# Strassen's scheme on eight slabs of the second column group of the down projections

## The chip, the cores and the metric

The kernel runs on one core of one Trainium2 chip. The metric is the device time of one execution in microseconds. TensorE is written PE (its weight loads PEld), VectorE DVE, ScalarE ACT, GpSimd POOL, and SyncE SP; SP only issues transfers here.

## The reference

Two transformer blocks over 256 tokens of width 2048, in float32. The first has a sparse attention and a gated recurrence, the second has two layers, a pooling mixer and a differential attention, and each of these two layers ends in the part that the change touches:

```python
def swiglu(h, w_gate, w_up, w_down):
    return (jax.nn.silu(h @ w_gate) * (h @ w_up)) @ w_down

def second_block(x, ...):
    for l in range(DEPTH_2):          # 2 layers
        ...
        h = rmsnorm(x, norm_ffn_pre[l])
        x = x + rmsnorm(swiglu(h, w_ffn_gate[l], w_ffn_up[l], w_ffn_down[l]), norm_ffn_post[l])
    return x
```

The hidden width is 5632, so that `w_down` is 5632 x 2048.

## The kernel before

**Tiling.** Every projection is cut into slabs of 1 MB of weights: 256 rows (two tiles of 128, `kt` = 2) by 1024 columns (two halves of 512). A stage (`Stage`) goes through its column groups, and in each through its slabs. A down projection (`down0`, `down1`, one per layer) has two column groups (0 and 1) of 22 slabs (0 to 21). The two token tiles and the two halves give four accumulators of 128 x 512 in PSUM, `acc`, with bank number 2t + n.

**Each slab** is fetched by SP in two transfers of 512 KB into one of `RING` = 5 slots of `raw`. ACT rounds it to the shorter format (`hi`, four slots, line 1486), DVE writes what is left (`lo`, line 2098) into the same place as `raw`, and signals `slab_split`. PE then makes three matmuls for each product (hi by hi, hi by lo, lo by hi; lines 808 to 810), 2 x 2 x 2 x 3 = 24 for a slab, and signals `slab_used`.

**Seven products in place of eight.** The slabs named in `SEVEN[g]` (3, 6, 9, 12, 15 in both groups) are multiplied by Strassen's scheme in Winograd's form: a slab is a 2 x 2 block of weights, the gated activations of its two row tiles and two token tiles another. DVE makes four sums of weight blocks (`weight_sums`, lines 2160 to 2163); three of them go into the next slot of the ring, as a slab of its own that nothing is fetched for (`"sums3"` and so on, 1536 columns wide). It also makes sums of the activations (`side_sums`, lines 2236 to 2241), which ACT rounds (`side_hi`) and DVE splits (`side_lo`, line 2246); they are made once, in group 0, and read again in group 1. PE runs 7 x 3 = 21 matmuls (`seven`, lines 1248 to 1250), 12 on the slab itself and 9 on the sums slab, partly into a second set of accumulators, `wk`.

**Mixing.** After the last such slab, DVE combines the four banks of `wk` (`mix_products`, lines 2252 to 2256) ahead of its conversion of slab 18, and adds the results into `acc` (`mix_into_acc`, lines 2263 and 2266) ahead of that of slab 19. For this PE leaves `acc` alone in turn: banks 2 and 3 rest from the end of slab 16 until the second half (t = 1) of slab 17, and banks 0 and 1 from the middle of slab 17 (signal `acc_paused`) until slab 18. PE waits for `acc_loaded` where it comes back.

**Order.** Each engine's program is a list written out by hand. DVE and ACT convert the slabs in the order of the list `slabs`, and SP fetches in that order (`RAWS`): the load of a slab waits until the slab five places earlier in the ring is used. Two transfers stand outside it: `keep_x` parks the residual x in DRAM, since the gate and up stages use its place, and `fetch_x` (line 700, two transfers of 1 MB) brings it back. It stands ahead of the load of slab 3 of group 0 of the down projection and waits for the last paired slab of the up stage. x is needed at the end of the down stage, when the normed result is added to it.

These are the loop that sets the order of the slabs, and the place of the fetch in SP's loop:

```python
            for s in range(2 if paired else 0, st.slabs):
                slabs.append((st, g, s))
                if st in st_down and s in SEVEN[g]:
                    slabs.append((st, g, f"sums{s}"))
...
            if st in st_down and (g, s) == (0, 3):
                fetch_x(st_down.index(st))
```

Of the kernel before, what the change touches and what calls it, by code (L numbers as in the profile page):

```python
# [39 lines left out]
SEVEN = ((3, 6, 9, 12, 15), (3, 6, 9, 12, 15))  # L40
# [56 lines left out]
def build(nc, t_in, out):  # L97
# [25 lines left out]
    SIDES_AT = (A0 + 8, A0 + 12, A0 + 4, A0 + 20, S0 + 1)  # L123
# [188 lines left out]
    for st in (st_rest, st_out, st_pool, st_gu[0], st_down[0], st_k, st_q, st_v, st_o, st_gu[1], st_down[1]):  # L312
        for g in range(st.groups):
            paired = st in st_gu and g >= CHAINED
            if paired:
                slabs += [(st, g, part) for part in "ABCD"]
            for s in range(2 if paired else 0, st.slabs):
                slabs.append((st, g, s))
                if st in st_down and s in SEVEN[g]:
                    slabs.append((st, g, f"sums{s}"))  # L320
# [34 lines left out]
    N_SIDES = len(SEVEN[0])  # L355
# [52 lines left out]
    MIX_DONE = max(SEVEN[0]) + 1  # L408
# [246 lines left out]
    def _(sp):  # L655
# [100 lines left out]
    def _(pe):  # L756

        def product(st, g, s, tokens=range(TT), between=None):
# [18 lines left out]
            for t in tokens:  # L777
                if st in st_down and (s, t) in ((MIX_DONE + 1, 1), (MIX_DONE + 2, 0)):
                    for n in range(2):
                        pe.wait_ge(acc_loaded[st.bank(t, n)], down_loaded(st_down.index(st), g, st.bank(t, n)))  # L780
                pauses = st in st_down and (s, t) in ((MIX_DONE, 1), (MIX_DONE + 1, 0))
                if st.lhs is not gt:
                    pe.wait_ge(h_ready, h_needed(st, k_end, t))
                for n in ([s] if st is st_pool else range(st.halves)):
# [8 lines left out]
                    for kk in range(st.kt):  # L793
# [13 lines left out]
                        loaded = (st.name, g, b) in LOADED or st in st_down and s > MIX_DONE + (t == 0)  # L807
# [429 lines left out]
        def seven(l, g, s):  # L1237

            st, i = st_down[l], SEVEN[0].index(s)
# [12 lines left out]
            first, last = s == min(SEVEN[g]), s == max(SEVEN[g])  # L1252
# [101 lines left out]
        def ffn(l):  # L1354
# [28 lines left out]
            for s in range(st_down[l].slabs - (2, 4)[l]):  # L1383
                down(l, 1, s)
# [78 lines left out]
    def _(act):  # L1463
# [586 lines left out]
    def _(vec):  # L2050
# [782 lines left out]
        def ffn(l):  # L2833
# [31 lines left out]
            for g in range(FG):  # L2865
# [155 lines left out]
    def _(pool):  # L3021
# [60 lines left out]
        pool.wait_ge(slab_used, number["down0", 0, MIX_DONE + 2] + 1)  # L3082
# [29 lines left out]
        pool.wait_ge(slab_used, number["down1", 0, MIX_DONE + 2] + 1)  # L3112
# [26 lines left out]
```

## Time and profile before

| | us |
|---|---|
| median of 3 runs | 2427.58 |
| lowest and highest | 2427.58, 2428.46 |
| the profiled execution, its time | 2428.43 |
| the profiled execution, its span | 2426.6 |
| PE busy | 2384.8 |
| DVE busy | 1973.3 |
| ACT busy | 1299.3 |
| mean granted PE clock | 0.996 |

The span runs from the first to the last instruction of the profile. Busy time is that of one engine, and engines overlap. In a timeline, a row is a group of like instructions one behind the other: its start, its length, the engine and line, the operation with output and input, the count, and in brackets how long the engine had been idle before it and what ended that. "DMA to landing" is the time from the issue of a transfer until its data are there. A matmul's listed length reaches past the start of the next one, because matmuls are pipelined.

### The profile page before, as it was taken

The numbers are of one execution on the slowest core, as the hardware profiler recorded it, in microseconds if no ns is written. First come the engines' busy times: TensorE is split into PE (matmuls) and PEld (weight loads), VectorE is DVE, ScalarE is ACT, GpSimd is POOL, SyncE is SP. The second block draws the span as 40 slices with busy tenths as digits, with TensorE's granted clock in tenths as the row PEclk, the third lists the DMA queues.
The fourth block names the chain that finished last, engine by engine and source line by source line (L and its number), as shares of the span: only waits on it lengthen the run. The fifth ranks groups of instructions, "written<-read, shape, count | busy, mean of one in ns | idle before, by whom it ended". The sixth has DMA issues, their size and how long they took to land.

```text
span 2426.6 us, 28811 instructions
## 1 busy us (share of the span) xinstructions
PE 2384.8 (98%) x11030; PEld 1979.5 (82%) x11030; DVE 1973.3 (81%) x2564; ACT 1299.3 (54%) x1703; POOL 99.0 (4%) x150
## 2 busy tenths in 40 slices
PE   5999999999999999999999999999999999999998
PEld 4888878888888888888888888888888888888887
DVE  6998988766889899897777768965699898988776
ACT  4757765445555555654444544554555555555443
POOL 0210000000000000000000212100000000000000
PEclk8999999999999999999999999999999999999999
DMA  9997665474566566566656655446666565565654
GB/s 383 360 385 246 240 208 171 166 262 167 192 208 208 191 208 196 186 199 215 229 188 205 196 196 193 160 142 203 218 210 200 188 212 188 195 222 189 224 191 156
DMA packets 190649, 515.46 MB, mean 212 GB/s; under 512 B 17920, under 2 KB 18208, under 8 KB 188208
## 3 DMA queue, kind: packets, MB, share of 16 engines
q1 hardware_dynamic: 178160, 465.31, 56.5%
q0 software_dynamic: 11824, 46.14, 5.1%
q8 instruction: 88, 1.44, 0.2%
q10 hardware_dynamic: 528, 2.16, 0.2%
q14 instruction: 49, 0.40, 0.0%
HBM read 507.26 MB, written 6.29 MB: 212 GB/s over the span
## 4 chain that ended last, share of the span: by engine, by line
PE 95%; DVE 2%; SPq 1%; DMA 0%; issue 0%; ACT 0%; DVEq 0%; ACTq 0%
PE acc L808 18%; PE acc L810 17%; PE acc L809 17%; PE acc L1276 4%; PE acc L1275 4%; PE acc L1277 4%; PE wk L1276 4%; PE wk L1275 4%; PE wk L1277 4%; PE acc L1317 1%; PE acc L1316 1%; PE acc L1318 1%; PE wk L1317 1%; PE wk L810 1%; PE wk L809 1%; PE wk L1316 1%
## 5 line engine op out<-in xcount | busy, mean ns | idle before, releaser
L2098 DVE TENSOR_TENSOR lo<-raw,hi 128x1024 fp32r<-128x1024 f32 (+2 forms) x428 | 486.8, 1188 | 110.2 <-ACT hi L1486 108.6
L1486 ACT ACTIVATE hi<-raw 128x1024 fp32r<-128x1024 f32 (+2 forms) x428 | 414.6, 1026 | 253.0 <-PE acc L810 122.1
L2100 DVE SCALAR_TENSOR_TENSOR lo<-raw,gcols,hi 128x1024 fp32r<-128x1024 f32 (+1 forms) x392 | 479.7, 1267 | 50.8 <-ACT hi L1486 48.3
L808 PE MATMUL acc<-hi,h 128*128 128x512 f32 x1312 | 519.4, 396 | 1.5 <-DVE lo L2098 0.5
L810 PE MATMUL acc<-hi,h 128*128 128x512 f32 x1312 | 511.7, 390 | 0.0
L809 PE MATMUL acc<-lo,h 128*128 128x512 f32 x1312 | 511.3, 390 | 0.0
L1486 ACT ACTIVATE hi<-raw,gcols 128x1024 fp32r<-128x1024 f32 (+1 forms) x392 | 416.6, 1124 | 140.4 <-PE acc L810 59.6
L808 PEld LDWEIGHTS acc<-hi,h 128*128 128x128 f32 x1312 | 246.8, 188 | 53.7 <-issue 2.7
L810 PEld LDWEIGHTS acc<-hi,h 128*128 128x128 f32 x1312 | 246.6, 188 | 52.3
L809 PEld LDWEIGHTS acc<-lo,h 128*128 128x128 f32 x1312 | 246.9, 188 | 49.1
L808 PE MATMUL acc<-hi,g_hi 128*128 128x512 f32 x544 | 211.9, 390 | 0.0
L810 PE MATMUL acc<-hi,g_lo 128*128 128x512 f32 x544 | 211.7, 389 | 0.0
L809 PE MATMUL acc<-lo,g_hi 128*128 128x512 f32 x544 | 211.6, 389 | 0.0
L1275 PE MATMUL acc<-hi,h 128*128 128x512 f32 x480 | 186.7, 389 | 0.0
L1276 PE MATMUL acc<-lo,h 128*128 128x512 f32 x480 | 186.7, 389 | 0.0
L1277 PE MATMUL acc<-hi,h 128*128 128x512 f32 x480 | 186.7, 389 | 0.0
L1275 PE MATMUL wk<-hi,h 128*128 128x512 f32 x400 | 155.6, 389 | 0.0
L1276 PE MATMUL wk<-lo,h 128*128 128x512 f32 x400 | 155.6, 389 | 0.0
L1277 PE MATMUL wk<-hi,h 128*128 128x512 f32 x400 | 155.6, 389 | 0.0
L2852 DVE STREAM_TRANSPOSE g_raw<-gated 32x256 f32<-32x256 f32 x320 | 139.4, 436 | 5.3
L810 PEld LDWEIGHTS acc<-hi,g_lo 128*128 128x128 f32 x544 | 102.1, 188 | 21.3
L809 PEld LDWEIGHTS acc<-lo,g_hi 128*128 128x128 f32 x544 | 102.1, 188 | 21.1
(445 smaller groups left out, 3403.8 us busy)
## 6 DMA issues: line engine op xcount, KB each, us to landing
raw<-in_w_ffn_gate SPq DMA_DIRECT2D x176, 512.0 KB, 3.8
raw<-in_w_ffn_up SPq DMA_DIRECT2D x176, 512.0 KB, 4.7
raw<-in_w_ffn_down SPq DMA_DIRECT2D x176, 512.0 KB, 4.7
raw<-in_w_in SPq DMA_DIRECT2D x144, 512.0 KB, 4.8
raw<-in_w_kv SPq DMA_DIRECT2D x64, 512.0 KB, 4.9
ada_raw<-in_ada_w POOLq DMA_DIRECT2D x38, 512.0 KB, 7.2
gate_raw<-in_ada_w POOLq DMA_DIRECT2D x32, 512.0 KB, 6.2
raw<-in_w_out SPq DMA_DIRECT2D x32, 512.0 KB, 4.8
```

The lines of the kernel that those rows point to most:

```text
L808: pe.matmul(o, l_hi, w_hi[:, c], start=first, stop=False, skip_group_check=loaded)
L809: pe.matmul(o, l_hi, w_lo[:, c], start=False, stop=False, skip_group_check=loaded)
L810: mm = pe.matmul(o, l_lo, w_hi[:, c], start=False, stop=last, skip_group_check=loaded)
L1275: pe.matmul(o, l_hi, w_hi, start=False, stop=False, skip_group_check=g >= CHAINED)
L1276: pe.matmul(o, l_hi, w_lo, start=False, stop=False, skip_group_check=g >= CHAINED)
L1277: mm = pe.matmul(o, l_lo, w_hi, start=False, stop=last, skip_group_check=g >= CHAINED)
L1316: pe.matmul(o, lhs[p][0], w_hi, start=first and p == 0, stop=False, skip_group_check=True)
L1317: pe.matmul(o, lhs[p][0], w_lo, start=False, stop=False, skip_group_check=True)
L1486: ins = act.activation(hi[:, m % HI_SLOTS, c], raw[:, r, c], ACT.Copy, scale=scale)
L2098: ins = vec.tensor_tensor(lo[:, r, c], raw[:, r, c], hi[:, m % HI_SLOTS, c], ALU.subtract)
L2100: ins = vec.scalar_tensor_tensor(out=lo[:, r, c], in0=raw[:, r, c], scalar=gcols[:, st.gain, k:k + 1], in1=hi[:, m % HI_SLOTS, c], op0=ALU ...
L2852: ins = vec.transpose(dst, src)
```

## The change

Group 1 of both down projections takes eight slabs by the seven-product scheme (1, 3, 6, 9, 12, 13, 14, 15) instead of five, and its slabs are run in another order, `DOWN_ORDER`, in which such slabs and ordinary ones alternate from position 0 to 15: 0, 1, 2, 3, 4, 6, 5, 9, 7, 12, 8, 13, 10, 15, 11, 14, and then 16 to 21. Group 0 keeps its slabs and order. The side sums of slabs 14, 1 and 13 are made in group 0 beside slabs 18, 20 and 21 (`LATE_SIDES`), and lie where x lies otherwise (`X0`, `X0 + 4`, `X0 + 8`). So `fetch_x` moves from slab 3 of group 0 to slab 17 of group 1, and waits until the sums slab of 14 is used; DVE waits for x later. The places of the mixing become a table (`MIX_AT`): as they were in group 0, and in group 1 the products ahead of the conversion of 17 and the additions ahead of that of 18.

```diff
-SEVEN = ((3, 6, 9, 12, 15), (3, 6, 9, 12, 15))
+SEVEN = ((3, 6, 9, 12, 15), (1, 3, 6, 9, 12, 13, 14, 15))
+LATE_SIDES = {18: 14, 20: 1, 21: 13}
+DOWN_ORDER = (0, 1, 2, 3, 4, 6, 5, 9, 7, 12, 8, 13, 10, 15, 11, 14, 16, 17, 18, 19, 20, 21)
+LAST_SEVEN = (15, 14)
+MIX_AT = ((16, 17, 18, 18, 19), (16, 17, 18, 17, 18))
...
-    SIDES_AT = (A0 + 8, A0 + 12, A0 + 4, A0 + 20, S0 + 1)
+    SIDES_AT = (A0 + 8, A0 + 12, A0 + 4, A0 + 20, S0 + 1, X0, X0 + 4, X0 + 8)
...
-            for s in range(2 if paired else 0, st.slabs):
+            for s in DOWN_ORDER if st in st_down and g else range(2 if paired else 0, st.slabs):
...
-            sp.wait_ge(slab_used, number[st_gu[l].name, FG - 1, "D"] + 1)
+            sp.wait_ge(slab_used, number[st_down[l].name, 1, "sums14"] + 1)
             for t in range(TT):
                 sp.dma_start(x[:, t], x_kept[:, t]).then_inc(x_fetched, 16)
...
-            if st in st_down and (g, s) == (0, 3):
+            if st in st_down and (g, s) == (1, 17):
                 fetch_x(st_down.index(st))
...
-                if st in st_down and (s, t) in ((MIX_DONE + 1, 1), (MIX_DONE + 2, 0)):
+                if st in st_down and (s, t) in ((MIX_AT[g][1], 1), (MIX_AT[g][2], 0)):
...
-                if g == 0 and s in SEVEN[0]:
-                    side_sums(l, SEVEN[0].index(s))
+                if sides_with(m) is not None:
+                    side_sums(*sides_with(m))
                 if s in SEVEN[g]:
                     weight_sums(m)
-                if s == MIX_DONE + 2:
+                if s == MIX_AT[g][3]:
                     mix_products(l, g)
-                if s == MIX_DONE + 3:
+                if s == MIX_AT[g][4]:
                     mix_into_acc(l, g)
...
-            vec.wait_ge(x_fetched, 16 * TT * (l + 1))
-            return m_evac(st_down[l], m_a, gain_a, (post_in, 16 * (l + 1)), 1 + 2 * l)
+            evac_down = m_evac(st_down[l], m_a, gain_a, (post_in, 16 * (l + 1)), 1 + 2 * l)
+            vec.wait_ge(x_fetched, 16 * TT * (l + 1))
+            return evac_down
```

SP, layer 0, from the end of the up stage to the next projection, in the kernel before (two rows of `w_ffn_down` are one slab):

```order
L688 DMA raw<-in_w_ffn_gate 128x2x512
L688 DMA raw<-in_w_ffn_up 128x2x512
L688 DMA raw<-in_w_ffn_down 128x1024 x6
L700 DMA x<-x_kept 128x2048 x2
L688 DMA raw<-in_w_ffn_down 128x1024 x82
L688 DMA raw<-in_w_kv 128x1024 x32
```

The same in the changed kernel:

```order
L706 DMA raw<-in_w_ffn_gate 128x2x512
L706 DMA raw<-in_w_ffn_up 128x2x512
L706 DMA raw<-in_w_ffn_down 128x1024 x78
L718 DMA x<-x_kept 128x2048 x2
L706 DMA raw<-in_w_ffn_down 128x1024 x10
L706 DMA raw<-in_w_kv 128x1024 x32
```

x moved from behind three slabs of the 44 to behind 39; the ten rows behind it are slabs 17 to 21 of group 1.

DVE, layer 0, end of group 1, in the kernel before: 16 and 17, the products of the mixing, 18, the additions, and 19 to 21 (`lo<-raw,hi 128x1024 x2` is the conversion of one slab):

```order
L2098 TENSOR_TENSOR lo<-raw,hi 128x1024 x4
L2252 COPY mixed_82<-wk 128x512
L2253 TENSOR_TENSOR mixed_83<-wk,mixed_82 128x512
L2254 TENSOR_TENSOR mixed_84<-wk,mixed_83 128x512
L2255 TENSOR_TENSOR mixed_85<-wk,mixed_83 128x512
L2256 TENSOR_TENSOR mixed_83<-wk,mixed_85 128x512
L2098 TENSOR_TENSOR lo<-raw,hi 128x1024 x2
L2263 TENSOR_TENSOR acc<-acc,mixed_85 128x512
L2263 TENSOR_TENSOR acc<-acc,mixed_83 128x512
L2266 TENSOR_TENSOR acc<-acc,mixed_82 128x512
L2266 TENSOR_TENSOR acc<-acc,mixed_84 128x512
L2098 TENSOR_TENSOR lo<-raw,hi 128x1024 x6
```

In the changed kernel:

```order
L2116 TENSOR_TENSOR lo<-raw,hi 128x1024 x2
L2270 COPY mixed_88<-wk 128x512
L2271 TENSOR_TENSOR mixed_89<-wk,mixed_88 128x512
L2272 TENSOR_TENSOR mixed_90<-wk,mixed_89 128x512
L2273 TENSOR_TENSOR mixed_91<-wk,mixed_89 128x512
L2274 TENSOR_TENSOR mixed_89<-wk,mixed_91 128x512
L2116 TENSOR_TENSOR lo<-raw,hi 128x1024 x2
L2281 TENSOR_TENSOR acc<-acc,mixed_91 128x512
L2281 TENSOR_TENSOR acc<-acc,mixed_89 128x512
L2284 TENSOR_TENSOR acc<-acc,mixed_88 128x512
L2284 TENSOR_TENSOR acc<-acc,mixed_90 128x512
L2116 TENSOR_TENSOR lo<-raw,hi 128x1024 x8
```

The conversion between products and additions was that of 18 and is that of 17; 18 now stands behind the additions.

DVE, layer 0, group 0, around the conversion of slab 18 (`side_r` is a split side set) in the kernel before:

```order
L2098 TENSOR_TENSOR lo<-raw,hi 128x1024 x4
L2252 COPY mixed_78<-wk 128x512
L2253 TENSOR_TENSOR mixed_79<-wk,mixed_78 128x512
L2254 TENSOR_TENSOR mixed_80<-wk,mixed_79 128x512
L2255 TENSOR_TENSOR mixed_81<-wk,mixed_79 128x512
L2256 TENSOR_TENSOR mixed_79<-wk,mixed_81 128x512
L2098 TENSOR_TENSOR lo<-raw,hi 128x1024 x2
L2263 TENSOR_TENSOR acc<-acc,mixed_81 128x512
```

In the changed kernel:

```order
L2254 TENSOR_TENSOR side_62<-g_hi,g_lo 128x512
L2256 TENSOR_TENSOR side_62<-side_62 128x128
L2257 TENSOR_TENSOR side_62<-side_62 128x128
L2258 TENSOR_TENSOR side_62<-side_62 128x128
L2259 TENSOR_TENSOR side_62<-side_62 128x128
L2270 COPY mixed_84<-wk 128x512
L2271 TENSOR_TENSOR mixed_85<-wk,mixed_84 128x512
L2272 TENSOR_TENSOR mixed_86<-wk,mixed_85 128x512
L2273 TENSOR_TENSOR mixed_87<-wk,mixed_85 128x512
L2274 TENSOR_TENSOR mixed_85<-wk,mixed_87 128x512
L2116 TENSOR_TENSOR lo<-raw,hi 128x1024 x2
L2264 TENSOR_TENSOR side_r_70<-side_62,side_r_70 128x512
```

A side set's five sums came ahead of the products, and its split between the conversion of 18 and the additions.

## Rows read from the trace of the kernel before

**Rows 1.** The page's first part: busy time, share, instructions by engine

```profile
PE 2384.8 (98%) x11030; PEld 1979.5 (82%) x11030; DVE 1973.3 (81%) x2564; ACT 1299.3 (54%) x1703; POOL 99.0 (4%) x150
```

**Rows 2.** The page's fourth part: the chain that ended last, by engine

```profile
PE 95%; DVE 2%; SPq 1%; DMA 0%; issue 0%; ACT 0%; DVEq 0%; ACTq 0%
```

**Rows 3.** Timeline of PE, layer 0, group 1: first matmuls of slabs 16, 17, 18

```profile
1300.58 0.39 PE L808 MATMUL acc<-hi,g_hi 128*128 128x512 f32 x1
...
1306.02 0.39 PE L808 MATMUL acc<-hi,g_hi 128*128 128x512 f32 x1
...
1311.46 0.39 PE L808 MATMUL acc<-hi,g_hi 128*128 128x512 f32 x1
```

**Rows 4.** Timeline of DVE, group 0: one seven-product slab with its side set

```profile
1136.25 0.69 DVE L2236 TENSOR_TENSOR side<-g_hi,g_lo 128x512 f32<-128x512 f32 x1
...
1138.03 0.68 DVE L2160 TENSOR_TENSOR raw<-raw 128x512 f32<-128x512 f32 x1
...
1143.08 0.69 DVE L2246 TENSOR_TENSOR side_r<-side,side_r 128x512 fp32r<-128x512 f32 x1
1143.68 4.09 DVE L2098 TENSOR_TENSOR lo<-raw,hi 128x768 fp32r<-128x768 f32 x4
```

**Rows 5.** SP's transfers by tile: lone slab, slab ahead of x, x, slab behind

```profile
L688 SPq DMA_DIRECT2D raw<-in_w_ffn_down x2: 328/328/328, 1249.1 to 1249.8; - x2
DMA to landing us min/median/max: 4.0/4.3/4.6
...
1089.05 0.80 SPq L688 DMA_DIRECT2D raw<-in_w_ffn_down  x2
...
L700 SPq DMA_DIRECT2D x<-x_kept x2: 430/472/513, 1089.9 to 1090.4; - x2
DMA to landing us min/median/max: 7.5/8.5/9.5
...
L688 SPq DMA_DIRECT2D raw<-in_w_ffn_down x2: 333/386/439, 1094.5 to 1094.9; - x2
DMA to landing us min/median/max: 6.7/7.1/7.5
```

**Rows 6.** Timeline of ACT and DVE: the conversion of one slab, group 1

```profile
1296.08 2.01 ACT L1486 ACTIVATE hi<-raw 128x1024 fp32r<-128x1024 f32 x2 [3.43 <-PE acc L810]
...
1297.17 2.36 DVE L2098 TENSOR_TENSOR lo<-raw,hi 128x1024 fp32r<-128x1024 f32 x2 [2.43 <-ACT hi L1486]
```

**Rows 7.** Timeline of DVE, layer 0, group 0: the mixing

```profile
1184.50 0.69 DVE L2252 COPY mixed<-wk 128x512 f32<-128x512 f32 x1 [1.25 <-PE acc L1250]
...
1188.12 2.36 DVE L2098 TENSOR_TENSOR lo<-raw,hi 128x1024 fp32r<-128x1024 f32 x2
1190.40 1.29 DVE L2263 TENSOR_TENSOR acc<-acc,mixed 128x512 f32<-128x512 f32 x2
1192.66 1.30 DVE L2266 TENSOR_TENSOR acc<-acc,mixed 128x512 f32<-128x512 f32 x2 [0.97 <-PE acc L810]
```

**Rows 8.** Timeline of DVE, layer 0, group 1: additions into banks 0 and 1

```profile
1308.94 1.30 DVE L2266 TENSOR_TENSOR acc<-acc,mixed 128x512 f32<-128x512 f32 x2 [0.97 <-PE acc L810]
```

**Rows 9.** Timeline of PE at the kernel's start

```profile
27.49 3.67 PE L929 MATMUL wk<-ident,xn 128*128 128x128 f32 x16 [5.48 <-ACT xn L1613]
39.31 3.57 PE L943 MATMUL acc<-ones,gate 128*128 128x1 f32 x16 [8.15 <-DVE gate L2072]
42.75 3.65 PE L929 MATMUL wk<-ident,xn 128*128 128x128 f32 x16
46.05 0.78 PE L808 MATMUL acc<-hi,h 128*128 128x512 f32 x1
...
48.60 0.40 PE L808 MATMUL acc<-hi,h 128*128 128x512 f32 x1
```

**Rows 10.** Windows of 1 us: each engine's busy time; granted clock third from last

```profile
34.00:35.00 1.00, 0.00 (x0) 0.00 (x0) 1.00 (x2) 0.00 (x0) 0.00 (x0) 0.86 1.00 406
```

More of the change, by code:

```diff
@@ L353, in gu_no, with sides_with @@
         return (FG - CHAINED) * l + g - CHAINED
-    N_SIDES = len(SEVEN[0])
+    SIDE_PAIRS = SEVEN[0] + tuple(LATE_SIDES.values())
+    N_SIDES = len(SIDE_PAIRS)
+    def sides_with(m):
+        st, g, s = slabs[m]
+        if st not in st_down or g:
+            return None
+        pair = s if s in SEVEN[0] else LATE_SIDES.get(s)
+        return None if pair is None else (st_down.index(st), SIDE_PAIRS.index(pair))
     DOWN_SIDES = [6 + l * (6 + 2 * N_SIDES) for l in range(2)]
@@ L407, in part_source, with mixed_in @@
         return raw_pair(lo if low else raw, st, g, q) if kind == "raw" else weight_sum(g, q, low)
-    MIX_DONE = max(SEVEN[0]) + 1
+    def mixed_in(g, s, t):
+        order = DOWN_ORDER if g else tuple(range(len(DOWN_ORDER)))
+        return order.index(s) > order.index(MIX_AT[g][1 - t])
     def gu_loaded(l, g, b):
@@ L777, in product @@
             for t in tokens:
-                if st in st_down and (s, t) in ((MIX_DONE + 1, 1), (MIX_DONE + 2, 0)):
+                if st in st_down and (s, t) in ((MIX_AT[g][1], 1), (MIX_AT[g][2], 0)):
                     for n in range(2):
                         pe.wait_ge(acc_loaded[st.bank(t, n)], down_loaded(st_down.index(st), g, st.bank(t, n)))
-                pauses = st in st_down and (s, t) in ((MIX_DONE, 1), (MIX_DONE + 1, 0))
+                pauses = st in st_down and (s, t) in ((MIX_AT[g][0], 1), (MIX_AT[g][1], 0))
                 if st.lhs is not gt:
@@ L806, in product @@
                         last = last or pauses and kk == st.kt - 1
-                        loaded = (st.name, g, b) in LOADED or st in st_down and s > MIX_DONE + (t == 0)
+                        loaded = (st.name, g, b) in LOADED or st in st_down and mixed_in(g, s, t)
                         pe.matmul(o, l_hi, w_hi[:, c], start=first, stop=False, skip_group_check=loaded)
@@ L1237, in seven @@
         def seven(l, g, s):
-            st, i = st_down[l], SEVEN[0].index(s)
+            st, i = st_down[l], SIDE_PAIRS.index(s)
             m = number[st.name, g, s]
@@ L1250, in add @@
                 return pe.matmul(o, lhs[1], w_hi, start=False, stop=last)
-            first, last = s == min(SEVEN[g]), s == max(SEVEN[g])
+            first, last = s == min(SEVEN[g]), s == LAST_SEVEN[g]
             pe.wait_ge(slab_split, m + 1)
@@ L1382, in ffn @@
                 down(l, 0, s)
-            for s in range(st_down[l].slabs - (2, 4)[l]):
+            for s in DOWN_ORDER[:st_down[l].slabs - (2, 4)[l]]:
                 down(l, 1, s)
@@ L1509, in conv_to @@
             while made[0] <= min(m, N_SLABS - 1):
-                if sevens(made[0]) is not None and slabs[made[0]][1] == 0:
-                    side_hi(sevens(made[0]), SEVEN[0].index(slabs[made[0]][2]))
+                if sides_with(made[0]) is not None:
+                    side_hi(*sides_with(made[0]))
                 conv(made[0])
@@ L2119, in conv_to @@
                 conv(made[0])
-                if sevens(made[0]) is not None and slabs[made[0]][1] == 0:
-                    side_lo(sevens(made[0]), SEVEN[0].index(slabs[made[0]][2]))
+                if sides_with(made[0]) is not None:
+                    side_lo(*sides_with(made[0]))
                 made[0] += 1
@@ L2228, in side_sums @@
         def side_sums(l, i):
-            s, gu = SEVEN[0][i], st_gu[l]
+            s, gu = SIDE_PAIRS[i], st_gu[l]
             a11, a21, a12, a22 = (side[i][:, 0, j, :] for j in range(4))
@@ L2250, in mix_products @@
             b = mixed[g]
-            vec.wait_ge(slab_used, number[st_down[l].name, g, f"sums{max(SEVEN[g])}"] + 1)
+            vec.wait_ge(slab_used, number[st_down[l].name, g, f"sums{LAST_SEVEN[g]}"] + 1)
             step(vec.tensor_copy(b[0][:], wk[:, 0, :]))
@@ L2260, in mix_into_acc @@
             b = mixed[g]
-            vec.wait_ge(slab_used, number[st_down[l].name, g, MIX_DONE] + 1)
+            vec.wait_ge(slab_used, number[st_down[l].name, g, MIX_AT[g][0]] + 1)
             for n, o in ((2, b[3]), (3, b[1])):
@@ L3080, in _ @@
         pool.dma_start(gain_g[:], t_in["norm_mix_post_2"][0:1, :].to_broadcast([P, D])).then_inc(pool_in, 16)
-        pool.wait_ge(slab_used, number["down0", 0, MIX_DONE + 2] + 1)
+        pool.wait_ge(slab_used, number["down0", 0, MIX_AT[0][2]] + 1)
         pool.dma_start(gain_a[:], t_in["norm_ffn_post_2"][0:1, :].to_broadcast([P, D])).then_inc(post_in, 16)
@@ L3111, in _ @@
         pool.dma_start(gain_g[:], t_in["norm_mix_post_2"][1:2, :].to_broadcast([P, D])).then_inc(mix1_in, 16)
-        pool.wait_ge(slab_used, number["down1", 0, MIX_DONE + 2] + 1)
+        pool.wait_ge(slab_used, number["down1", 0, MIX_AT[0][2]] + 1)
         pool.dma_start(gain_a[:], t_in["norm_ffn_post_2"][1:2, :].to_broadcast([P, D])).then_inc(post_in, 16)
```

## The prediction, made before the changed kernel had run

> **What bounds the kernel now.** I read the busy shares first: PE works for 2384.8 of 2426.6 us [rows 1]. The chain that ended last says the same: 95% of it is PE's own [rows 2]. So a matmul less is worth its place in PE's stream, and every wait of PE is paid in full. Then I read PE's stream at the changed place, to have both prices. A matmul is listed with 0.39 us, but that is its length, not its place: slab 16 of column group 1 starts at 1300.58 and slab 17 at 1306.02, 24 matmuls in 5.44 us, so one costs 0.227 us [rows 3]. An ordinary slab is 5.44 us, a seven-product slab (21 matmuls) 4.76 us. PE has no gap in the down stages of this trace; the question is whether the edit makes one.
>
> I count from T, the start of position 16 in group 1 (here 1300.58), in one layer, and double at the end, since both layers carry the same tables. The profiled execution took 2428.43 us with a span of 2426.6; the median of the runs is 2427.58. The sum is a difference against the profiled span, and I add it to the median.
>
> **What it removes.** Group 1 goes from five to eight seven-product slabs, three matmuls less in each of three: 9 x 0.227 = 2.04 us a layer, 4.08 us in all. That is 0.17%, and a measurement of this kernel can tell about 0.2% from no change: even with nothing lost, the gain is too small to be called faster.
>
> **What it adds on DVE, pair by pair.** In group 1 a seven-product slab now alternates with an ordinary one, PE 10.20 us a pair. DVE needs for the pair the four sums and the low part, 1138.03 to 1143.08 = 5.05 us, then the low parts of the sums slab and of an ordinary slab, 4.09 us [rows 4]: 9.14 us. It fits, with 1 us to spare in each pair. The ring of five raw slots is the other limit: an ordinary slab of a pair is asked for when the seven-product slab two pairs earlier has given its slot back, 12.2 us before PE wants it. A lone slab lands about 5.3 us after its first request (1249.1 to 1249.8 + 4.6) [rows 5], and needs 1.09 us until DVE starts behind ACT (1296.08 to 1297.17) and 2.36 us of DVE [rows 6], 8.75 us in all. About 3.5 us are left. I cost the pairs at nothing; if this cover were gone, each missing microsecond would be paid up to eight times a layer.
>
> **The late sides in group 0.** Three side sets are added, ahead of slabs 18, 20 and 21. One costs DVE 1.78 us for the sums (1136.25 to 1138.03) and 0.60 for the low part (1143.08 to 1143.68) [rows 4]. Those at 20 and 21 lie in slack: from 1194.1 on, three conversions and the two sets are some 11.7 us, which ends at 1205.8, and PE starts 21 four slabs after 17, at about 1211.5. The one at slab 18 stands ahead of the mixing. DVE had 1.25 us idle there, so the products begin 0.5 us later, and with 0.60 more behind the conversion of 18 the first additions into acc end 1.1 us later: 1190.40 + 1.29 + 1.1 = 1192.8 [rows 7]. PE wants these two banks at about 1192.45 (the pause signal released DVE at 1192.66, and it is given at the end of a matmul whose successor starts 0.2 us before). I take 0.4 us of PE wait; bounds 0 and 0.6.
>
> **The fetch of x, the term that decides.** It moves on SP from slab 3 of group 0 to just ahead of slab 17 of group 1, and it now waits until the sums slab of 14 is used, which is T + 0.2. SP issues in order. Queued behind this wait are the loads of 17, 18, 19, 20 and 21. The slot for 17 has been free since the start of the pair (11, 14), 10.2 us before T, so the wait throws away all of the load's lead. Then x's 2 MB are asked for ahead of 17's 1 MB. The nearest rows are x's own fetch in the kernel before: a slab asked for at 1089.1, x at 1089.9 and 1090.4, its second half landing 9.5 us later at 1099.9 [rows 5]. That is 3 MB, one slab and x, 10.85 us after the first request. The new order has the same 3 MB, only x first. So 17 lands at T + 11.05, has its high and low part 1.09 + 2.36 us later, and PE can start it at T + 14.55 instead of T + 5.44: **9.1 us idle**. Bounds: from 5.3 us for a lone slab plus 2 x 2.5 us, the spacing in which x's halves and the slab behind them landed (1097.4, 1099.9, 1102.4) [rows 5], 10.3 us and 8.55 idle; and from 12.5 us (x's first request to the landing of the slab behind it, with a slab ahead of it as well), 10.75 idle. Who waits besides: ACT and DVE stand at the conversion of 17, and PE at its product.
>
> The Trainium skill ("DMA: Bandwidth & Descriptors", section "Two DMAs through the same engine are not ordered") says that within one queue of one engine descriptors start in order, and that nothing orders transfers across the 16 engines. By the first half 17 waits for x; by the second it could slip past x in part. The trace agrees with the first half: the slab asked for behind x, at 1094.5, landed 7.5 us after its second request, against 4.6 for a lone one [rows 5].
>
> **Mixing one step earlier in group 1.** The additions into acc now stand ahead of the conversion of 18, not of 19. Banks 0 and 1 can be added only once PE has paused in the middle of 17, and 18's low part is behind them: 1308.94 + 1.30 + 2.36 = 1312.6, less 0.1 where they overlap, and PE wants 18 at 1311.46 [rows 3, 8]. **1.1 us idle**, wherever 17 starts, since both ends hang on it; bounds 0.8 and 1.3. The products before 17 take some 3.6 us and lie under the wait for 17's load.
>
> **The clock.** In the kernel before PE went idle for 8.15 us ahead of 39.31, and the granted clock fell from full to half in the window 34 to 35 (0.86 of it granted), some 3.6 us after the last matmul; an idle time of 5.48 us ahead of 27.49 had left it at full [rows 9, 10]. An idle time of 9.1 us is on the far side of both. At 1.2 GHz the matmuls from 46.05 on take 0.43 instead of 0.227 us; the six up to 48.60 took 2.55 instead of 1.36 us, 1.2 us lost, and dense work had been under way there since 42.75, which would make 2.85 us if it were all 512 columns. I take 2.0 us per stall, nearer to the middle of these; bounds 0 (it stays at full) and 2.85. The Trainium skill ("TensorE: Matmul & The Clock Gate", section "What's actually happening") calls the half rate the default from which activity frees the array; rows 10 agree.
>
> **Sum.** -2.04 + 0.4 + 9.1 + 1.1 + 2.0 = +10.56 us a layer, +21.1 in both: 2427.6 + 21.1 = **2448.7 us**. With all low ends 2427.6 + 2 x 7.3 = 2442.2, with all high ends 2427.6 + 2 x 13.5 = 2454.6.
>
> **Rivals.**
> (a) x does not stand in 17's way: its packets move beside or behind 17's. The wait alone is left: 17 lands at T + 0.2 + 5.3, starts at T + 9.0, 3.6 us idle, the clock stays up (under 5.48 us idle). -2.04 + 0.4 + 3.6 + 1.1 = +3.1 a layer, 2433.7. For it: DMA queues are shared by 16 engines. Against it: the slab behind x did come late in the kernel before.
> (b) Not slower: 17 is ready in time. It would have to land by T + 1.9, so within 1.7 us of its request, or be asked for by T - 3.2; the order of SP rules out the second and rows 5 the first. Then only the mixing costs: -2.04 + 0.4 + 1.1, 2426.5, or 2423.5 if that is free too. A gain of over 0.2% needs something that the trace does not show.
> (c) The pairs fall behind: DVE or the ring misses by over 1 us a pair once the 3.5 us are eaten. With 1 us in each of the last five pairs, +5 a layer on top of the forecast, 2459.
> (d) 17's load is spread among those of 18, 19 and 20, which are asked for right behind it (their slots are free by T). With 6 MB, the first at the lone slab's 5.3 us and five at 2.78 (10.85 less 5.3, halved), 17 lands up to 8.3 us later: 2465 at the worst; in part it is inside my range.
>
> **Chances.** Forecast 0.76, (a) 0.08, (b) 0.05, (c) 0.05, (d) 0.06. The range of 2437 to 2457 takes in both bounds of the sum with some microseconds to spare, and leaves out (a), (b) and the far ends of (c) and (d). Slower by over 0.2% (above 2432.4) 0.93, within 0.2% 0.05, faster 0.02.
>
> **What would show it.** PE waits twice a layer in group 1: about 9 us at the first product of 17, released by DVE's low part behind a DMA of w_ffn_down, and about 1 us at 18. SP's two x requests stand within 0.3 us of the end of the sums slab of 14. The granted clock dips after the long wait. PE's 11030 matmuls become 11012. No other new wait of PE exceeds 0.5 us. Wrong would be: 17 landing before T + 9, a wait of under 7 us at 17, or waits inside the pairs at positions 1 to 15.

## The result and the profile after

| | before | after |
|---|---|---|
| median, us | 2428.02 | 2451.01 |
| lowest and highest of 4 runs, us | 2427.58, 2428.96 | 2449.27, 2452.2 |
| span of the profiled execution, us | 2426.6 | 2450.0 |
| PE busy, us | 2384.8 | 2386.6 |
| DVE busy, us | 1973.3 | 2012.9 |
| mean granted PE clock | 0.996 | 0.995 |

The changed kernel takes 1.0094 times as long, with an interval of 1.0082 to 1.0105. That is 23.0 us more than before; the prediction was 2448.7 with a range of 2437 to 2457.

First the busy times and the engines of the chain that ended last, in the profile after. They answer [rows 1, 2].

```profile
PE 2386.6 (97%) x11012; PEld 1977.7 (81%) x11012; DVE 2012.9 (82%) x2636; ACT 1309.7 (53%) x1721; POOL 99.2 (4%) x150
...
PE 92%; DVE 4%; DMA 2%; ACT 1%; issue 1%; SPq 0%; DVEq 0%; ACTq 0%
```

PE runs the 18 matmuls less that the tables promise, yet is busy for longer: some ran at half rate. The rest of the loss isn't busy time. It stands in PE's waits (columns: total us, times, longest us), of which the kernel before had 0.5 us once for the low part and none in the down stages:

```profile
PE acc L826 <- DVE lo L2116: 20.8, 5, 9.3
...
PE acc L826 <- DVE acc L2281: 0.7, 2, 0.4
```

PE's timeline shows where they are. Layer 0, group 1, the starts of 17 and of 18, then of 17 in layer 1; they answer [rows 3]:

```profile
1313.94 0.80 PE L826 MATMUL acc<-hi,g_hi 128*128 128x512 f32 x1 [9.23 <-DVE lo L2116]
1314.54 0.63 PE L827 MATMUL acc<-lo,g_hi 128*128 128x512 f32 x1
...
1323.06 0.50 PE L826 MATMUL acc<-hi,g_hi 128*128 128x512 f32 x1 [0.92 <-DVE lo L2116]
...
2410.17 0.80 PE L826 MATMUL acc<-hi,g_hi 128*128 128x512 f32 x1 [9.30 <-DVE lo L2116]
```

Each layer has one long wait at slab 17 and a short one at slab 18. The low part is named, but DVE only passes the delay on. ACT's row of the same slab names what stands behind it, and SP's rows when that was asked for: x first, then the ten transfers of slabs 17 to 21. The two `raw` requests of the last rows are slab 17's.

```profile
1310.37 2.00 ACT L1504 ACTIVATE hi<-raw 128x1024 fp32r<-128x1024 f32 x2 [15.73 <-DMA raw<-in_w_ffn_down]
...
1299.30 0.80 SPq L718 DMA_DIRECT2D x<-x_kept  x2
1300.15 5.46 SPq L706 DMA_DIRECT2D raw<-in_w_ffn_down  x10
...
L706 SPq DMA_DIRECT2D raw<-in_w_ffn_down x2: 430/578/725, 1300.1 to 1300.6; - x2
DMA to landing us min/median/max: 8.1/8.9/9.7
```

The second half of 17 landed at 1300.6 + 9.7 = 1310.3, 11.0 us after x's first request. The granted clock is the third number from the right in the windows of 1 us:

```profile
1308.00:1309.00 1.00, 0.00 (x0) 0.00 (x0) 0.00 (x0) 0.00 (x0) 0.00 (x0) 1.00 0.92 205
1309.00:1310.00 1.00, 0.00 (x0) 0.00 (x0) 0.00 (x0) 0.00 (x0) 0.00 (x0) 0.52 0.98 344
...
1317.00:1318.00 1.00, 1.00 (x4) 0.71 (x4) 0.00 (x0) 0.47 (x2) 0.00 (x0) 0.50 1.03 422
1320.00:1322.00 2.00, 2.00 (x10) 1.45 (x8) 2.00 (x4) 0.00 (x0) 0.00 (x0) 1.00 0.00 0
```

It falls to half, 1.2 GHz, while PE is idle, and stays there for the first matmuls of 17. These stand 0.427 us apart, 12 of them in layer 0 and 11 in layer 1. Against 0.227 us that is 2.4 and 2.2 us lost.

### The profile page after: what moved, and what is told of

The parts are those of the page before. It is cut to its first block, busy times and chain, and to the rows that moved or that the text cites. A ratio compares the mean times of both kernels' runs of the same rounds, so it can differ in the third digit from the quotient of the medians.

```text
span 2450.0 us, 28887 instructions
## 1 busy us (share of the span) xinstructions
PE 2386.6 (97%) x11012; PEld 1977.7 (81%) x11012; DVE 2012.9 (82%) x2636; ACT 1309.7 (53%) x1721; POOL 99.2 (4%) x150
## 4 chain that ended last, share of the span: by engine, by line
PE 92%; DVE 4%; DMA 2%; ACT 1%; issue 1%; SPq 0%; DVEq 0%; ACTq 0%
PE acc L826 16%; PE acc L828 16%; PE acc L827 16%; PE acc L1295 4%; PE acc L1294 4%; PE acc L1293 4%; PE wk L1295 4%; PE wk L1294 4%; PE wk L1293 4%; PE acc L1336 1%; PE acc L1335 1%; PE acc L1334 1%; PE wk L1334 1%; PE wk L1336 1%; PE wk L828 1%; PE wk L826 1%
## 5 line engine op out<-in xcount | busy, mean ns | idle before, releaser
L2116 DVE TENSOR_TENSOR lo<-raw,hi 128x1024 fp32r<-128x1024 f32 (+2 forms) x440 | 498.0, 1182 | 109.4 <-ACT hi L1504 107.6
L1504 ACT ACTIVATE hi<-raw 128x1024 fp32r<-128x1024 f32 (+2 forms) x440 | 422.7, 1020 | 249.3 <-PE acc L828 74.6
L826 PE MATMUL acc<-hi,g_hi 128*128 128x512 f32 x496 | 196.0, 395 | 21.1 <-DVE lo L2116 20.3
L827 PE MATMUL acc<-lo,g_hi 128*128 128x512 f32 x496 | 194.8, 393 | 0.0
L828 PE MATMUL acc<-hi,g_lo 128*128 128x512 f32 x496 | 194.7, 393 | 0.0
L826 PEld LDWEIGHTS acc<-hi,g_hi 128*128 128x128 f32 x496 | 94.3, 190 | 43.0 <-DVE lo L2116 22.0
L1522 ACT ACTIVATE hi<-t 128x1024 fp32r<-128x1024 f32 x72 | 74.3, 1056 | 81.5 <-DVE t L2198 65.0
```

Of the source, the lines that this page charges most:

```text
L826: pe.matmul(o, l_hi, w_hi[:, c], start=first, stop=False, skip_group_check=loaded)
L827: pe.matmul(o, l_hi, w_lo[:, c], start=False, stop=False, skip_group_check=loaded)
L828: mm = pe.matmul(o, l_lo, w_hi[:, c], start=False, stop=last, skip_group_check=loaded)
L1504: ins = act.activation(hi[:, m % HI_SLOTS, c], raw[:, r, c], ACT.Copy, scale=scale)
L1522: act.activation(dst, part_source(st, g, kind, q), ACT.Copy).then_inc(hi_made, 2 if part == "D" else 1)
L2116: ins = vec.tensor_tensor(lo[:, r, c], raw[:, r, c], hi[:, m % HI_SLOTS, c], ALU.subtract)
```

## The account of the 23.4 us between the spans

| | us |
|---|---|
| 18 matmuls less, 0.227 each | -4.1 |
| waits at 17: 9.23 and 9.30 | +18.5 |
| waits at 18: 0.92 and 0.90 | +1.8 |
| waits for the additions in group 0 | +0.7 |
| half clock: 2.4 and 2.2 | +4.6 |
| sum | +21.5 |

Some 1.9 us are left. Most of them are the price of a wait in place, which is higher than the idle time listed. It is best read in a kernel without any clock loss, the experiment e10 below, PE around its wait at slab 17:

```profile
1306.48 0.39 PE L810 MATMUL acc<-hi,g_lo 128*128 128x512 f32 x1
1307.51 0.50 PE L808 MATMUL acc<-hi,g_hi 128*128 128x512 f32 x1 [0.64 <-DVE lo L2098]
1307.85 0.40 PE L809 MATMUL acc<-lo,g_hi 128*128 128x512 f32 x1
```

From start to start it is 1.03 us where it would be 0.227, so 0.80 for a listed 0.64: the idle time counts from the end of a length of 0.39, which is 0.16 more than the matmul's place. The next start is 0.34 instead of 0.227 behind. A wait thus costs its listed time plus 0.27, and six waits 1.6 us. The last 0.3 us isn't traced; the first down stage began anywhere between 1098.9 and 1101.0 in the profiles of all these kernels, so single spans differ by that much ahead of any edit.

## Experiments

Times are medians; each ratio is against the kernel before, run on the same chip, with its interval. That median is 2428.42 us for e1, e4, e5 and e6, 2427.92 for e2, e3 and e7, and 2428.34 for e8, e9 and e10. The intervals reach 2 to 4 us to either side, so medians that lie closer than that are told apart here only by the waits in their traces. The theory: the loss is the late load of 17 behind x, plus the clock that the idle time costs, plus the mixing moved ahead of 18; the pairs at positions 1 to 15 are free. The rivals: x's volume doesn't matter, only SP's wait; the pairs or the side sets cost time of their own; the mixing is what costs.

**e1: x fetched behind slab 21.** The wait of SP and x's transfers no longer stand ahead of 17; the mixing stays early.

```diff
-            if st in st_down and (g, s) == (1, 17):
-                fetch_x(st_down.index(st))
...
+            if st in st_down and (g, s) == (1, 21):      # behind the two loads of the slab
+                fetch_x(st_down.index(st))
```

> The changed kernel with one thing different: x is fetched behind the load of slab 21 of group 1, not ahead of that of slab 17 (it still waits for the sums slab of 14, which is over by then). Theory A, the queue of SP is what costs: PE's wait of 9.2 to 9.3 us at slab 17 goes in both layers and the clock stays at full; left are the waits of 0.35 us (group 0) and 0.9 us (slab 18) a layer, each 0.16 us dearer in place than listed. 2428.0 - 4.1 + 2 x 1.6 = 2427.1. Theory B, the denser order of the slabs (pairs, late sides) costs as well, hidden behind the long wait: 2430 or more, with PE waits at positions 1 to 15. Theory C, x is now late for the last addition: DVE waits for a DMA of x before line 2763, and 2430 or more.

Measured: 2430.13 us (2428.21 to 2430.9), ratio 1.0005 (0.9996 to 1.0014). 21 of the 23 us are gone and the clock stays at full (1.00 in every window of 1 us from 1300 to 1314), so the fetch's place is the cause of the loss. The expectation was missed by 3 us, since 17 still waits. PE at 17 and 18, and DVE ahead of that:

```profile
1304.80 0.50 PE L826 MATMUL acc<-hi,g_hi 128*128 128x512 f32 x1 [0.64 <-DVE lo L2116]
...
1311.50 0.50 PE L826 MATMUL acc<-hi,g_hi 128*128 128x512 f32 x1 [0.93 <-DVE lo L2116]
...
1298.76 0.69 DVE L2270 COPY mixed<-wk 128x512 f32<-128x512 f32 x1 [2.27 <-PE acc L1268]
1302.39 2.36 DVE L2116 TENSOR_TENSOR lo<-raw,hi 128x1024 fp32r<-128x1024 f32 x2
```

DVE has no idle time between the products of the mixing and the conversion of 17: the products can start only when the last seven-product slab is through PE, and their 3.6 us push the conversion past the moment at which PE wants it. In the changed kernel this lay under the wait for the load. The sum fits: -4.1, waits 2 x (0.64 + 0.93), 0.5 in group 0, and 6 x 0.27 give +1.2; the median says +1.7.

**e10: the early mixing alone.** In the kernel before, five slabs in group 1 and x's fetch where it was:

```diff
-                if s == MIX_DONE + 2:
+                if s == MIX_DONE + 2 - g:
                     mix_products(l, g)
-                if s == MIX_DONE + 3:
+                if s == MIX_DONE + 3 - g:
                     mix_into_acc(l, g)
```

> The kernel before with one other part alone: in group 1 the products of the mixing ahead of the conversion of 17 and the additions ahead of that of 18. Slabs, order, sides and the fetch of x are as before. If the additions ahead of 18's conversion cost what they did in the changed kernel, PE waits 0.9 us at 18 in both layers, 1.2 us in place, and up to 0.6 us at 17, where the products now stand ahead of 17's conversion: 2428.2 + 2.4 to 2428.2 + 4. If they cost only with the new order, 2428.

Measured: 2432.06 us (2431.48 to 2434.68), ratio 1.0016 (1.0006 to 1.0025). Its PE has the same two waits as e1, 0.64 and 0.93 us, in both layers; with 0.27 each for the four, that is 4.2 us, and 3.7 were measured, inside the expected range. So of the 5.8 us by which e1 misses a clean gain of 4.1, some 4 are the mixing's place. Another 1.0 are the two waits in group 0, which e10 doesn't have; the last 0.6 are within what these medians leave open. Neither the pairs nor x is needed to explain it.

**e4: e1 with the mixing late again.**

```diff
-MIX_AT = ((16, 17, 18, 18, 19), (16, 17, 18, 17, 18))
+MIX_AT = ((16, 17, 18, 18, 19), (16, 17, 18, 18, 19))
```

> As the kernel with x fetched last, and the mixing of group 1 back where it was (products ahead of the conversion of 18, additions ahead of that of 19). If the wait at 18 comes from the additions standing ahead of 18's conversion, it goes, and 2 x 1.1 us with it: 2425.0. If 18 is late for another reason (its load), the wait stays and the time is that of x fetched last, 2427.1.

Measured: 2425.67 us (2424.84 to 2426.93), ratio 0.9987 (0.9978 to 0.9996). The expectation of 2425.0 was met within 0.7. The waits at 17 and 18 are gone in both layers, and the pairs run through without one. In layer 0 PE still starts the second half of slab 17 some 0.3 us late, too little to be listed as a wait. What is left of listed new waits is in group 0, where the late side set of 14 stands ahead of the mixing:

```profile
1193.39 0.47 PE L826 MATMUL acc<-hi,g_hi 128*128 128x512 f32 x1 [0.27 <-DVE acc L2281]
```

**e5: the side set of 14 beside slab 17.** e4 with one number changed, to take the set out of the mixing's way:

```diff
-LATE_SIDES = {18: 14, 20: 1, 21: 13}
+LATE_SIDES = {17: 14, 20: 1, 21: 13}
```

> As the one before it (x last, mixing of group 1 late), and the side set of slab 14 made ahead of slab 17 of group 0 instead of 18, where DVE stood idle for 1.76 us behind ACT. If the 0.35 us in group 0 come from the side set between the mixing's steps, they go: 2425.0 - 2 x 0.5 = 2424.0, and PE waits nowhere in the down stages. That is 4.0 us under the kernel before, the bare worth of 18 matmuls. If DVE is behind already there, 2425 or more.

Measured: 2426.11 us (2423.89 to 2427.34), ratio 0.9989 (0.998 to 0.9998). No gain over e4; the expectation of 2424.0 was missed. The side set moved, and the delay came along: PE waits for the additions for 0.58 us in group 0 of layer 1, where e4 had 0.26, and in layer 0 it starts 0.3 us late there. DVE, group 0:

```profile
1180.24 0.68 DVE L2254 TENSOR_TENSOR side<-g_hi,g_lo 128x512 f32<-128x512 f32 x1
...
1183.75 2.36 DVE L2116 TENSOR_TENSOR lo<-raw,hi 128x1024 fp32r<-128x1024 f32 x2 [1.65 <-ACT hi L1504]
1186.03 0.69 DVE L2264 TENSOR_TENSOR side_r<-side,side_r 128x512 fp32r<-128x512 f32 x1
1186.63 0.68 DVE L2270 COPY mixed<-wk 128x512 f32<-128x512 f32 x1
```

ACT rounds the side set ahead of the slab itself, and it can only do so once DVE has made the sums; so DVE makes the sums and then idles for 1.65 us until ACT comes to the slab. Such a set costs DVE 1.78 + 1.65 + 0.60 = 4.0 us, not 2.4. In the changed kernel the sets at 20 and 21 show the same 1.65 us; the one at 18 doesn't, since the products of the mixing fill that time.

**e8: the side set behind the additions, the slab ahead of it on ACT.** e4 with

```diff
-LATE_SIDES = {18: 14, 20: 1, 21: 13}
+LATE_SIDES = {19: 14, 20: 1, 21: 13}
...
-                if sides_with(made[0]) is not None:
+                st, g, s = slabs[made[0]]
+                late = s in LATE_SIDES
+                if not late and sides_with(made[0]) is not None:
                     side_hi(*sides_with(made[0]))
                 conv(made[0])
+                if late and sides_with(made[0]) is not None:
+                    side_hi(*sides_with(made[0]))
...
+                if s == MIX_AT[g][4]:
+                    mix_into_acc(l, g)
                 if sides_with(m) is not None:
                     side_sums(*sides_with(m))
...
-                if s == MIX_AT[g][4]:
-                    mix_into_acc(l, g)
```

> As the kernel with x fetched last and the mixing of group 1 late (2425.7), but the side set of slab 14 stands at slab 19 of group 0, behind the additions into acc, and for the three late sets ACT rounds the slab first and the side set second. Moving the set to 17 had failed because the slab's high part stood behind the set's on ACT, which left DVE idle for 1.65 us in each late set. If that reading holds, PE's gap at slab 17 of group 0 (0.5 us of place a layer) goes, DVE has no idle time of 1.65 us at the late sets, and the time is 2425.7 - 1.0 = 2424.7. If DVE has simply too much to do there, a wait of PE turns up at slabs 19 to 21 instead.

Measured: 2424.13 us (2423.45 to 2425.5) against 2428.34, ratio 0.9984 (0.9975 to 0.9993). PE has no new wait left, and the 4.2 us are the removed matmuls (18 x 0.227 = 4.1). This version is faster than both kernels, by 0.16% against the kernel before, and the time is 0.6 under the expected 2424.7. DVE, group 0, from the additions through the first of the three late sets:

```profile
1192.27 1.30 DVE L2287 TENSOR_TENSOR acc<-acc,mixed 128x512 f32<-128x512 f32 x2 [0.97 <-PE acc L828]
1193.48 0.68 DVE L2257 TENSOR_TENSOR side<-g_hi,g_lo 128x512 f32<-128x512 f32 x1
...
1195.26 2.36 DVE L2119 TENSOR_TENSOR lo<-raw,hi 128x1024 fp32r<-128x1024 f32 x2
1197.53 0.69 DVE L2267 TENSOR_TENSOR side_r<-side,side_r 128x512 fp32r<-128x512 f32 x1
```

The additions stand as close behind the products as in [rows 7], with no set ahead of them, and the 1.65 us of idle time are gone.

**e6: five slabs in group 1.** e5 with the three extra slabs taken back, in the same order of slabs and with the late side sets still made (the wait of x for the sums slab of 15 isn't shown):

```diff
-SEVEN = ((3, 6, 9, 12, 15), (1, 3, 6, 9, 12, 13, 14, 15))
+SEVEN = ((3, 6, 9, 12, 15), (3, 6, 9, 12, 15))
-LAST_SEVEN = (15, 14)
+LAST_SEVEN = (15, 15)
```

> As the one before it, but group 1 has its five old seven-product slabs (3, 6, 9, 12, 15) at the places of the new order; slabs 1, 13 and 14 are ordinary, their side sets are still made, and x waits for the sums slab of 15. This measures the gain of the three slabs by itself: 18 matmuls more, 2424.0 + 4.1 = 2428.1. If the scheme's gain is eaten by its sums and slots, the difference is under 2 us; if a matmul cost its listed 0.39 us it would be 7.0.

Measured: 2429.05 us (2428.22 to 2429.52), ratio 1.0001 (0.9992 to 1.001), 2.9 us above e5 where 4.1 were expected, with intervals of 2.2 us to either side of both. Sharper is the stretch within the traces from the first matmul of the down stage to ACT's first reading of group 1's result, in layer 0: 227.69 us in e6, 225.59 in e5. The 2.10 us in a layer are the 9 matmuls at 0.227 (2.04); at their length of 0.39 it would be 3.5.

**e2: SP waits, x doesn't stand ahead of 17.** The changed kernel with x at the end as in e1, but SP still waiting for the sums slab of 14 ahead of the load of 17. This is rival (a) of the prediction made real.

```diff
             if st in st_down and (g, s) == (1, 17):
-                fetch_x(st_down.index(st))
+                sp.wait_ge(slab_used, number[st.name, 1, "sums14"] + 1)
...
+            if st in st_down and (g, s) == (1, 21):
+                fetch_x(st_down.index(st))
```

> The changed kernel, but only SP's wait for the sums slab of 14 stands ahead of the load of 17; x itself is fetched behind slab 21. It measures the wait without the bytes. If SP's queue costs by the wait and by x's bytes one after the other, 17 lands 5.3 us after its request (9.7 to 10.9 in the changed kernel), PE is idle 3.5 us at 17 and the clock stays at full: with 0.9 and 0.35 left, 2427.1 + 2 x 3.6 = 2434.3. If the bytes alone matter, 2427. If the wait alone matters, 2451.

Measured: 2442.3 us (2442.14 to 2442.77), ratio 1.0058 (1.0041 to 1.0075), 8 us above what was expected. PE at 17 in the two layers:

```profile
1309.62 0.50 PE L828 MATMUL acc<-hi,g_hi 128*128 128x512 f32 x1 [4.50 <-DVE lo L2118]
...
2400.28 0.79 PE L828 MATMUL acc<-hi,g_hi 128*128 128x512 f32 x1 [4.65 <-DVE lo L2118]
```

and two windows of layer 0 just behind the wait, then one inside the wait of layer 1:

```profile
1309.00:1310.00 1.00, 0.38 (x2) 0.34 (x3) 1.00 (x2) 1.00 (x2) 0.00 (x0) 1.00 1.03 422
1310.00:1311.00 1.00, 1.00 (x4) 0.79 (x3) 0.77 (x2) 0.51 (x1) 0.00 (x0) 0.60 1.03 422
...
2399.00:2400.00 1.00, 0.00 (x0) 0.00 (x0) 1.00 (x2) 0.85 (x1) 0.00 (x0) 0.53 1.00 410
```

The idle time is nearly as expected; the clock is not. In layer 0 it fell after PE had already restarted, and about 8 matmuls ran at half rate (1.6 us); in layer 1 it fell during the wait, and about 13 did (2.6 us). The sum: -4.1, waits 9.15 at 17, 1.7 at 18 and 0.5 in group 0, 6 x 0.27, and 4.2 of clock give +13.1; measured +14.4. The last 1.3 us isn't traced.

**e3: one of x's two transfers ahead of 17.** As the changed kernel, but `fetch_x` for one token tile at 17 and for the other behind 21 (the function takes the tile as its second argument):

```diff
-                fetch_x(st_down.index(st))
+                fetch_x(st_down.index(st), 0)
...
+            if st in st_down and (g, s) == (1, 21):
+                fetch_x(st_down.index(st), 1)
```

> The changed kernel, but one of x's two transfers (1 MB) stays ahead of the load of 17 and the other goes behind slab 21. 17 lands 2.1 to 2.8 us later than with the wait alone, PE is idle 5.6 to 6.3 us. It also brackets the clock between the 5.48 us that left it at full and the 8.15 us that did not. With the clock at full 2434.3 + 2 x 2.5 = 2439; with the clock falling 2 us more a layer, 2443.

Measured: 2445.17 us (2443.79 to 2446.04), ratio 1.0068 (1.0053 to 1.0083). PE at 17:

```profile
1310.66 0.80 PE L827 MATMUL acc<-hi,g_hi 128*128 128x512 f32 x1 [6.64 <-DVE lo L2117]
```

That is 2.2 us above the expected 2443. The idle time is 0.3 us over its upper bound (6.3 us), because e2's wait, from which it was counted, is itself a microsecond longer than expected. The clock fell in both layers, but only 7 matmuls ran at half rate in each (some 1.4 us).

With e2 and the changed kernel this is a ladder: 4.5, 6.6 and 9.2 us idle with none, one and two transfers of 1 MB ahead of the slab. x's bytes do stand in 17's way, 2.1 and 2.6 us a MB, and the wait alone is a bit under half of the stall.

**e9: SP waits for slab 14 itself.** The slab itself, the first part of the last seven-product pair, is used 9 matmuls (2.0 us) ahead of its sums slab; the rest is as in e2.

```diff
             if st in st_down and (g, s) == (1, 17):
-                fetch_x(st_down.index(st))
+                sp.wait_ge(slab_used, number[st.name, 1, 14] + 1)
```

> The changed kernel with x fetched last, and ahead of the load of 17 a wait for the first part of slab 14, which ends 2.0 us before that of its sums slab. It asks how short an idle time of PE costs the clock: 4.5 us did (the wait for the sums slab), where 5.48 us at the kernel's start did not. PE should be idle 2.5 us at 17. If the clock stays at full, 1.8 us a layer more than with x last: 2430.1 + 3.7 = 2433.8. If it falls here too, 1.6 to 2.7 us a layer more: 2437 to 2439.

Measured: 2436.8 us (2436.32 to 2437.6), ratio 1.0036 (1.0022 to 1.0049). PE at 17 and its clock:

```profile
1306.56 0.79 PE L828 MATMUL acc<-hi,g_hi 128*128 128x512 f32 x1 [2.74 <-DVE lo L2118]
1307.15 0.63 PE L829 MATMUL acc<-lo,g_hi 128*128 128x512 f32 x1
...
1304.00:1305.00 1.00, 0.00 (x0) 0.00 (x0) 0.85 (x1) 0.99 (x2) 0.00 (x0) 1.00 1.02 418
1306.00:1307.00 1.00, 0.44 (x1) 0.44 (x2) 1.00 (x2) 1.00 (x2) 0.00 (x0) 0.80 1.03 422
1308.00:1309.00 1.00, 1.00 (x4) 0.80 (x3) 0.00 (x0) 1.00 (x2) 0.00 (x0) 0.50 1.01 414
```

The time is 0.2 us under the range expected for a falling clock. Even 2.74 us of idle time cost the full clock, for about 8 matmuls (1.5 us) here, and 2.61 us cost as much in layer 1.

**e7: the fetch moved alone.** The kernel before, five slabs, late mixing, with x's fetch ahead of 17 as in the changed kernel (DVE's later wait for x isn't shown):

```diff
-            sp.wait_ge(slab_used, number[st_gu[l].name, FG - 1, "D"] + 1)
+            sp.wait_ge(slab_used, number[st_down[l].name, 1, "sums15"] + 1)
...
-            if st in st_down and (g, s) == (0, 3):
+            if st in st_down and (g, s) == (1, 17):
                 fetch_x(st_down.index(st))
```

> The kernel before with one part of the change alone: x is fetched ahead of slab 17 of group 1, behind a wait for the last sums slab (15 there), and DVE waits for x where the changed kernel does. Slabs, order, sides and mixing are as before. If the loss is that of the fetch alone, it shows here in full: PE idle 9.2 us at 17 and half clock for 2.2 us' worth a layer, 2428.0 + 2 x 11.6 = 2451. If it needs the shorter leads of the new order, it is under half of that, 2428 to 2440.

Measured: 2458.6 us (2457.6 to 2459.73), ratio 1.0124 (1.0109 to 1.014), 7.6 above what was expected. PE in layer 1:

```profile
2413.67 0.80 PE L808 MATMUL acc<-hi,g_hi 128*128 128x512 f32 x1 [9.21 <-DVE lo L2098]
...
2420.87 0.77 PE L808 MATMUL acc<-hi,g_hi 128*128 128x512 f32 x1 [2.69 <-DVE acc L2263]
```

The long wait is the same. The second one (1.71 us in layer 0) is for the additions. With the late mixing they stand behind the products and the conversion of 18, and DVE has no idle time from the late conversion of 17 up to them. In layer 0:

```profile
1312.90 2.36 DVE L2098 TENSOR_TENSOR lo<-raw,hi 128x1024 fp32r<-128x1024 f32 x2 [18.51 <-ACT hi L1486]
...
1318.80 2.36 DVE L2098 TENSOR_TENSOR lo<-raw,hi 128x1024 fp32r<-128x1024 f32 x2
1321.08 1.29 DVE L2263 TENSOR_TENSOR acc<-acc,mixed 128x512 f32<-128x512 f32 x2
```

The changed kernel's 2451.0, the 18 matmuls that e7 still runs (4.1) and second waits of 4.4 in place of 1.8 us make 2457.7. Against that, e7 has no waits in group 0 (1.2 us in place), and in layer 1 its second wait cost the clock again, 14 matmuls at half rate in all where the changed kernel has 11 (0.6 us): 2457.1. The early mixing avoids the second wait and pays 0.9 in its place. So the two edits interact. With x fetched ahead of 17 the early mixing is the better one; with x out of the way it costs 3.7 us (e10) and the late one is free (e4).

## Why the prediction was right

**What bounds the kernel, and the price of a matmul**: right. Every wait was paid in full, and 9 matmuls were worth 2.10 us a layer (e6 against e5) where 2.04 was the term. The Trainium skill ("TensorE: Matmul & The Clock Gate", section "Wait — 56ns, not 53.3ns?") gives 426.7 ns from start to start at N = 512 with the array cold and 215.7 ns warm. The first agrees with the 0.427 us after the stalls; at full clock these traces show 0.227, and the term went by that.

**x ahead of 17**: right, the term that decided. 9.1 us were worked out, 9.23 and 9.30 measured; 17 landed 11.0 us after x's first request, 10.85 were taken. e1 shows that the place of the fetch is the cause, and e3 that the bytes count as well as the wait.

**The additions ahead of 18**: 1.1 worked out, 0.92 and 0.90 listed, 1.2 with the price in place.

**Group 0**: 0.4 worked out, 0.35 a layer listed. Its mechanism holds (e8 removes it).

**The clock**: 2.0 worked out, 2.4 and 2.2 measured. It fell during the wait, where the prediction had looked for the fall behind it.

**The pairs at nothing**: right. PE has no new wait at positions 1 to 15 in any of the versions, and e8 brings the whole gain. Rival (c) didn't occur, and (d) not in its strong form: 17 landed only 0.15 us later than worked out. That its load can lose some time with others asked for behind it is open (see (a) below).

**Too low by 2.3 us**: 0.4 of it is the median before (2428.0 for 2427.6), and the change was 23.0 where 21.1 had been worked out. The sum priced each wait at its idle time. With 0.27 more for each of six waits it would be 1.6 us higher.

Mis-sized without effect on the time were three other steps:

- The late side sets at 20 and 21 cost DVE 4.0 us each, not 2.4. The conversion of 21 ended at 1208.4, not 1205.8, still ahead of PE.
- Rival (a) was priced at 2433.7, and made real (e2) it gives 2442.3. The step that failed is "the clock stays up (under 5.48 us idle)". The 5.48 us of [rows 9] lay between groups of small matmuls at the kernel's start and were no bound for the idle time at 17; why the clock stayed up there, no run shows. The load of 17 also took 6.3 us, from 1299.72 to ACT's start on it at 1306.05, with four more slabs asked for behind it, where 5.3 had been taken from a lone slab; whether those slabs took the 1 us wasn't tried.
- Rival (b), 17 ready in time, was priced at 2426.5 with only the 1.1 us at 18. e1 is that case and took 2430.13: the products ahead of 17 cost a wait of their own as soon as no load hides them. The prediction had named that cover ("lie under the wait for 17's load") but not said what they cost without it. Its second price, 2423.5 with the mixing free, also leaves out the 0.4 of group 0; with that it would be 2424.3.

In the term for x, T + 11.05 + 1.09 + 2.36 is T + 14.50, not 14.55, which changes nothing.

Open is the rest of some 0.3 us in the account.

## What to carry to other kernels

A transfer that waits for a late event, put into an in-order queue, holds back every load behind it. Its price is what the lost lead of those loads no longer covers (4.5 us of idle time here) plus the bytes queued ahead of them (2.1 and 2.6 us a MB), so it belongs behind the last prefetch of its stage (here 21 of 23 us came back). Check the cover of each edit against the version in which its neighbour is repaired: the early mixing was hidden by the late load, better than the late one beside it, and cost 3.7 us once it was alone. Price a wait of a saturated PE at its listed idle time plus 0.27 us, and plus the clock if it is 2.6 us or longer (1.3 to 2.6 us a stall here).

## What the runs showed of the hardware

How idle times of PE went with the granted clock here:

| idle before the matmul, us | where | at half clock afterwards |
|---|---|---|
| 0.64, 0.93 | e1, e10: slabs 17, 18 | nothing |
| 2.74, 2.61 | e9, both layers | about 8 matmuls, 1.5 us each |
| 4.50 | e2, layer 0 | about 8 matmuls, 1.6 us; fell after PE's restart |
| 4.65 | e2, layer 1 | about 13 matmuls, 2.6 us |
| 6.64, 6.56 | e3, both layers | 7 matmuls, 1.4 us each |
| 9.23 | after, layer 0 | 12 matmuls, 2.4 us |
| 9.30 | after, layer 1 | 11 matmuls, 2.2 us |
| 9.42 | e7, layer 0 | 12 matmuls, 2.4 us, up to the next wait |
| 9.21 | e7, layer 1 | 7 matmuls, 1.4 us |
| 2.69 | e7, layer 1, second wait | about 7 matmuls, 1.3 us |
| 5.48 | kernel's start [rows 9] | none seen |

The length of the idle time alone doesn't tell the loss: 4.50 and 4.65 us cost 1.6 and 2.6, 6.6 us cost 1.4, and the four of over 9 us between 1.4 and 2.4. Unexpected was that 2.61 us are enough, and that the clock can fall while PE is back at work. It can also rise while PE is idle: in layer 0 of e7 it was at half before the second wait and at full again ahead of the restart at 1322.51.

```profile
1320.00:1321.00 1.00, 0.81 (x2) 0.09 (x1) 1.00 (x2) 1.00 (x2) 0.00 (x0) 0.50 0.69 283
1321.00:1322.00 1.00, 0.00 (x0) 0.00 (x0) 1.00 (x3) 0.34 (x1) 0.00 (x0) 0.89 0.04 16
```

Where between 0.93 and 2.61 us the loss begins wasn't tried.
